# Weight pieces in two buffers instead of three, gathered rows in nine slots instead of eight

## What is computed

```python
h = _rmsnorm(x, norm1_g)
z = jnp.einsum("btd,de->bte", h, w_in)          # 1024 -> 6664: q, k, v of two attentions, forget logits, gates
oa_ = _diff_attn(qa_, ka_all, va_all, ...)      # 8 heads, two maps each
ob_ = _fox_attn(qb_, kb_all, vb_all, ...)       # 8 heads with decay
merged = gates[:, :, 0] * (oa @ w_pa) + gates[:, :, 1] * (ob @ w_pb)
x = x + merged @ w_o
# PEER: 16 experts for each of 8 heads, out of 16384
q = xb @ wq                                      # 1024 -> 2048
sc = q . subkeys;  two top-16 lists, their 256 sums, top-16 of these -> eidx, g = softmax
act = gelu(u[eidx] . xb)
x = x + sum((g * act) * v[eidx])
y = _rmsnorm(x, final_g)
```

## Time and profile before

| | us |
|---|---|
| median of 3 runs | 2340.24 (2328.39 to 2342.65) |
| profiled execution, its own time | 2342.73 |
| its span in the profile | 2340.6 |
| PE busy | 1789.7 (76%) |
| DVE busy | 1507.2 (64%) |
| POOL busy | 748.3 (32%) |
| ACT busy | 592.7 (25%) |
| gathers, share of the 16 DMA engines | 61.4% |
| weights and the rest of SP's queue | 18.4% |

### The profile page before, as it was taken

One profiled execution on the slowest core, in us unless ns is written; L12 is line 12 of the kernel. 1 busy time (PEld: TensorE's weight loads), 2 busy tenths in 40 slices (PEclk: granted clock), 3 DMA queues, 4 the chain that ended last, 5 costly groups with the idle time before them and its releaser, 6 DMA issues. The chain is left out here.

```text
span 2340.6 us, 22944 instructions
## 1 busy us (share of the span) xinstructions
PE 1789.7 (76%) x7392; PEld 1081.7 (46%) x7392; DVE 1507.2 (64%) x3478; ACT 592.7 (25%) x1631; POOL 748.3 (32%) x697
## 2 busy tenths in 40 slices
PE   7889898799876866776787767858777787787655
PEld 6855674456644652343663324436532333563210
DVE  0021209686675469786758977756698887659956
ACT  3232011311152122343013325411222353013211
POOL 0000000544423123343334543322445344235532
PEclk9998999899987997888899899878998898899988
DMA  7842654999898787889999998899999889999977
GB/s 236 300 148 67 201 195 142 405 422 414 305 387 305 289 325 257 331 322 371 377 383 420 376 367 305 305 396 391 418 413 373 314 316 343 399 386 382 367 316 305
DMA packets 139303, 765.00 MB, mean 327 GB/s; under 512 B 18608, under 2 KB 42464, under 8 KB 52016
## 3 DMA queue, kind: packets, MB, share of 16 engines
q0 software_dynamic: 78336, 570.46, 61.4%
q1 hardware_dynamic: 27632, 161.42, 18.4%
q10 hardware_dynamic: 33216, 31.67, 4.1%
HBM read 744.77 MB, written 18.30 MB: 326 GB/s over the span
## 5 line engine op out<-in xcount | busy, mean ns | idle before, releaser
L645 POOL DMA_INDIRECT ring<-in_uv,stage x544 | 687.3, 1263 | 1138.7 <-PE acc L1275 438.5
L1275 PE MATMUL acc<-ring,diag 128*128 128x512 f32 (+1 forms) x1268 | 677.6, 683 | 248.0 <-DVE diag L1611 130.3
L1600 DVE CUSTOM_DVE_ANT_0 ring<-ring,xb 128x1024 f32<-128x1024 f32 x544 | 645.5, 1220 | 79.5 <-DMA ring<-in_uv,stage 62.7
L1275 PEld LDWEIGHTS acc<-ring,diag 128*128 128x128 f32 (+1 forms) x1268 | 254.9, 212 | 624.4 <-issue 278.3
L923 ACT ACTIVATE gel<-dots 128x1 f32<-128x1 f32 x544 | 100.6, 199 | 852.0 <-DVE dots L1600 842.0
L1625 DVE SCALAR_TENSOR_TENSOR vsum<-ring,coefd,vsum 128x1024 f32<-128x1024 f32 x222 | 285.4, 1286 | 8.1 <-DVE coefd L1618 0.2
L1037 PE MATMUL pz<-F,wbuf 128*128 128x416 f32 (+1 forms) x656 | 240.8, 526 | 25.4 <-ACT F L782 20.0
L665 POOL COPY stage<-idx 128x4 int32<-128x4 int32 x136 | 58.2, 428 | 424.5 <-DVE gw L1556 404.5
L1037 PEld LDWEIGHTS pz<-F,wbuf 128*128 128x128 f32 (+1 forms) x656 | 124.6, 193 | 137.6 <-issue 137.6
L1618 DVE TENSOR_SCALAR coefd<-gel,gw 128x1 f32<-128x1 f32 x227 | 47.5, 209 | 166.6 <-ACT gel L923 166.1
L1611 DVE TENSOR_SCALAR diag<-ident,gel,gw 128x128 f32<-128x128 f32 x159 | 55.0, 356 | 95.3 <-ACT gel L923 93.2
(11 more groups left out here) (299 smaller groups left out, 2092.2 us busy)
## 6 DMA issues: line engine op xcount, KB each, us to landing
wbuf<-in_w_z SPq DMA_DIRECT2D x52, 1024.0 KB
wbuf<-in_w_q SPq DMA_DIRECT2D x40, 1024.0 KB
wbuf<-in_w_pa SPq DMA_DIRECT2D x20, 1024.0 KB
wbuf<-in_w_o SPq DMA_DIRECT2D x20, 1024.0 KB
wbuf<-in_w_pb SPq DMA_DIRECT2D x20, 512.0 KB
ring<-in_uv,stage POOLq DMA_INDIRECT x544
zT<-F ACTq DMA_DIRECT2D x28, 208.0 KB, 5.2
wbuf<-in_w_sk SPq DMA_DIRECT2D x5, 1024.0 KB
```

Of the source, the lines that this page charges most:

```text
L645: pool.indirect_dma_start(out=ring[:, slot, :], out_offset=None, in_=d["uv"], in_offset=bass.IndirectOffsetOnAxis(ap=stage[:, a, k:k + 1], ...
L1275: last = nc.tensor.matmul(acc[0:nq, c * 512:(c + 1) * 512], diag[:, parity, 0:nq], ring[:, slot, D + c * 512:D + (c + 1) * 512], start=Fal ...
L1600: nc.vector.tensor_tensor_reduce(out=u, in0=u, in1=xb[:, t % 2, :], scale=1.0, scalar=0.0, op0=ALU.mult, op1=ALU.add, accum_out=dots[:, sl ...
```

## The change

One buffer less for weights (`wbuf` gets 8 KB smaller in each partition), one buffer more in the ring (8 KB larger). Both numbers stand in the formulas that were shown: the semaphores, the buffer of a piece or slot and the waits follow from them.

```diff
 PC = 16
 CW = 256
-WBUFS = 3
-RING = 8
+WBUFS = 2
+RING = 9
 BLOCK = 4
 HALF = BLOCK // 2
```

## The result

| | before | after |
|---|---|---|
| median, us | 2334.31 (4 runs, 2324.04 to 2342.65) | 2504.62 (4 runs, 2495.98 to 2506.69) |
| profiled execution, us | 2342.73 | 2495.98 |
| PE's mean granted clock in it | 0.901 | 0.872 |

The ratio of after to before is 1.0707, with a 95% interval of 1.0672 to 1.0741: 170 us more by the medians, 153 by the two profiled executions, of which that of before was the slowest of its runs and that of after the fastest. The forecast was +91.

The account below looks back on a forecast made before the run. No engine alone sets the pace; weights are tight in the bursts, rows ample. Terms 24 + 34 + 28 + 16 + 2 - 13 = +91 gave 2434 us, 2431 us as median; range 2365 to 2505.

Parts of the forecast that it names:

- The bound: Whole kernel: weights are tight in the bursts, where a buffer goes; rows are ample, DVE waiting only 62.7 us for them.
- (a): Group 0, pieces 9 to 26, ahead of the first gather: nine pairs take 82.8 us instead of 74.0, +7.
- (b): Tile 0's two bursts, without gathers beside them: +13 for the first, +4 for the second.
- (c): First bursts of tiles 1 to 4, 202 us in all before: +34, with +14 and +84 as its bounds.
- (d): Second bursts of tiles 1 to 4: +7 us each, +28 for four (+4 to +60).
- (e): PE's clock falling after the new waits in the bursts of tiles 1 to 4: 0 to 63 us, taken as +16.
- L: Time from issue to landing of a weight load alone in SP's queue: 7.5 us in bursts, bounds 6 and 9.5.
- (f): Group 1's 17 pieces beside tile 0's experts: loads hidden with 2 us to spare; 0 to +14, taken as +2.
- (g): The ninth ring slot: one more gather done beforehand in each of five stretches with DMA full, 2.6 us each, -13.
- Rival 1: A lone weight load keeps half of the bandwidth beside gathers and lands in 6 us: +29, 2369 us; chance 0.20.
- Rival 2: Loads take 9.5 us in bursts too, two thirds of the pairs at low clock: +202, 2542 us; chance 0.10.
- Rival 3: Not slower: full DMA engines set the time, the nine-slot ring hands time back behind bursts: +11, 2351 us; chance 0.10.

## Why the prediction was right, and too small

**The bound.** That weights are tight and rows ample held: the buffer's removal made all of the loss, and an additional slot at most 16 us of gain.

**(a) and (b), ahead of the first gather.** +24 forecast, +35.7 measured. Group 0 ended 15 us later instead of 7: the first eight pieces cost 3.5, which I had at nothing, and some of its loads landed later than the 5.2 us that I had for all. Tile 0's bursts grew by 17.2 and 8.6 instead of 13 and 4, and what lies between them, attention above all, gave some 5 back. There, too, the clock was the missing piece. PE's timeline of tile 0's first burst, against the earlier trace rows:

```profile
273.88 5.47 PE L1196 MATMUL acc<-ring,wbuf 128*128 128x128 f32 x32 [2.80 <-DMA wbuf<-in_w_pa]
279.49 2.02 PE L1205 MATMUL acc<-ring,wbuf 128*128 128x128 f32 x16
284.20 5.47 PE L1196 MATMUL ps<-ring,wbuf 128*128 128x128 f32 x32 [2.69 <-DMA wbuf<-in_w_pa]
```

The load takes 4.85 us (279.35 to 284.20), better than my 5.2, but the piece 5.47 instead of 3.81. The pair is 10.3 us instead of 9.2.

**(c) and (d), the bursts.** +62 forecast, +138 measured together with (e), for which I had +16: 60 us too little. The step L = 7.5 us was right: the loads for which the 36 pairs of tiles 1 to 4 wait take 7.6 us on average, between 4.8 and 10.4. The "4.0" in "two pieces take L + 4.0" was wrong. It stands for the piece that follows the wait, and in 29 of the 36 pairs that piece ran at the lower clock for a part of it, 5.2 to 6.7 us for a w_pa or w_q. The 36 pairs take 480 us, 13.3 each, which is 7.6 + 5.7. The 1.7 us more are 61 us in 36 pairs, where (e) allowed 16: 45 of the 60 us. The second error is tile 1: "few gathers beside it", L = 5.5; the loads of its first burst took 7.1 us, which is 8 us more for five pairs. The last 7 us are longer loads in the other bursts, above all in tile 3's first one, where they took 8.5.

**(e), the clock**, is then the term that was mis-sized. I had it as a sum of its own with a quarter of its bound and argued from pieces that went at full length after waits of 1.1 us; the new waits were 2.5 to 8 us, and nearly all the pieces behind them were slow. The bound of +63 contained it. How the loss divides between landing and clock is read from the traces (97 us more of waits for weights in these bursts, 42 us more of busy time than before, when some pieces were slow already); the run with the clock kept up shows no more than its lower bound of some 20 us.

**(f)**, group 1's pieces beside tile 0's experts: hidden, as forecast. None of them waits for a landing, their releasers in the view of lines being ACT and PE.

**(g)**, the ninth slot, -13: 6 us by the pair of runs at two buffers, and 7 us less of row wait between them (54.8 to 47.5; the rest of the way from 62.7 came with the lost buffer, before the slot). The intervals of the two runs leave room for 6 and for 13, so that the term is neither confirmed nor refuted.

**The rivals.** Rival 1, a lone load with half of the bandwidth, fell: L was 7.6, not 6. From 1286.7 to 1295.5 of the changed kernel, in tile 2's second burst, a load takes 8.8 us, and the weights get 1.28 MB beside 2.29 of the gathers:

```profile
q0 software_dynamic: 312, 2.29, 63.9%
q1 hardware_dynamic: 172, 1.28, 36.1%
```

In some stretches ACT's queue (q10) takes a part too. The stretch of the earlier trace rows was one, which the prediction didn't say: ACT's queue had 211 packets there, so that its 9.5 us need not be the price of gathers alone. From 1654.9 to 1665 of the changed kernel the weights moved 1.16 MB, the gathers 2.41:

```profile
q0 software_dynamic: 326, 2.41, 57.6%
q1 hardware_dynamic: 172, 1.16, 27.9%
q10 hardware_dynamic: 322, 0.65, 16.9%
...
wbuf<-in_w_pa SPq DMA_DIRECT2D x1, 1024.0 KB, 10.0
```

Rival 2 was wrong in its L of 9.5 and right that most pairs would meet a low clock (29 of 36, where it had two thirds); its 13.5 us from pair to pair are near the 13.3 measured, by a longer load and a shorter piece than in truth. Rival 3 fell: attention kept its length, and what came back behind the bursts was some 20 us, within the 62.7 us of row waits. The measured time lies at the upper edge of the range because (c) came out at its upper bound, 84 us, by another route than the one that had set it. The direction and the path were forecast rightly, but that the median is within the range at all, by 0.4 us, is luck: 170 us lie nearer to rival 2's 202 than to the 91 forecast, and outside of the 2390 to 2480 that I had given to the forecast itself.

## What to carry to other kernels

The number of buffers for a stream that is loaded piece by piece follows from two durations in the trace, the landing from its issue *beside the other traffic* and the work on the piece between; where the first is longer than the second, the third buffer is on the path, and its price is counted once for each pair of pieces. Add to each such wait the slower matrix multiplications behind it. When memory is short, cut the pieces, each with its own landing and its own release, and not their number: four halves lost 1.3% where two wholes lost 7%, in the same bytes. To cut the load alone, with one wait and one release for all of its parts, made it worse.

## What the hardware showed that I had not expected

- Waits of 2.7 to 2.8 us in tile 0 of the changed kernel were each followed by 32 matrix multiplications that took 5.47 us instead of 3.81, at a granted clock of 0.69 in that stretch; before, waits of 1.1 us left them at 3.84. The length of the wait doesn't decide it alone: in the kernel before, 2.03 us were followed by a piece of 5.47 us, and 2.91 us (tile 4's first burst; timeline, then clock, DMA share and GB/s of the stretch) by one at the full clock:

```profile
2021.03 3.84 PE L1196 MATMUL pz<-F,wbuf 128*128 128x128 f32 x32 [2.91 <-DMA wbuf<-in_w_pa]
...
2021.03:2024.87 3.84, 3.84 (x32) 1.00 1.02 417
```

- Four small loads in place of a large one are later, alone and beside gathers: 6.2 us instead of 5.1 for a piece in tile 0's bursts; later on the same piece as four loads with rows of 2 KB was waited for up to 17.0 us, as one load with rows of 8 KB up to 8.4.
- Halving the bytes of every gather shortened the loads for which the pairs wait only from 7.6 to 6.7 us on average (5.1 without gathers), and two buffers then cost 190 us instead of 170.
